# Time-step logits of an SSD layer with the weights stationary, head squares summed on VectorE, and gate outputs evacuated ahead of weight splits, in a three-layer float32 forward pass on one core

## The reference, cut to what matters

```python
# layer 1: short convolution gate, SSD, memory attention (x: 1 x 256 x 2048)
proj = rms_norm(x, norm_w) @ w_in
sc_b, sc_c, sc_v, sc_z, ssd_z, ssd_xbc, ssd_dt, mq, mz = _split(proj, EVEN_SPLITS)
y_a = sc_b * causal_depthwise_conv(sc_c * sc_v, sc_conv_w) * jax.nn.silu(sc_z)
dt = jax.nn.softplus(ssd_dt + ssd_dt_bias)          # 256 x 32: the time steps
y_b = ssd_chunked(xs, dt, -exp(ssd_a_log), bm, cm) + xs * ssd_d
y_b = group_rms_norm(y_b * silu(ssd_z)) * ssd_norm_w     # mean square over 512 columns
y_m = memory_attention(mq, mem_n, w_mk, w_mv) * silu(mz)
x = x + concatenate([y_a, y_b, y_m]) @ w_out
# layer 2: MLA (latent attention), then the first block's final norm
# layer 3: retention, 8 heads of 512 value columns
q, k, v, g = split(rmsnorm(x) @ w_in)
o = scores(q, k) * decay @ v
o = head_norm(o, gain, center=True) * silu(g)       # mean square over 512 columns, per head
x = x + o @ w_out
x = x + square(relu(rmsnorm(x) @ w_up)) @ w_down
return rmsnorm(x)
```

## Time and profile before

| | |
|---|---|
| median of 3 runs | 2830.67 us (2828.84 to 2835.06) |
| profiled execution, its own time | 2829.0 us |
| its span, first to last instruction | 2827.5 us |
| busy: PE, DVE, ACT | 98%, 69%, 50% of the span |
| mean granted TensorE clock | 0.992 of full |

### The profile page before, as it was taken

One profiled execution on the slowest core, in us unless ns is written; L12 is line 12 of the kernel. 1 busy time (PEld: TensorE's weight loads), 2 busy tenths in 40 slices (PEclk: granted clock), 3 DMA queues, 4 the chain that ended last, 5 costly groups with the idle time before them and its releaser, 6 DMA issues.

```text
span 2827.5 us, 46051 instructions
## 1 busy us (share of the span) xinstructions
PE 2759.5 (98%) x15758; PEld 2394.6 (85%) x15758; DVE 1956.2 (69%) x3098; ACT 1412.8 (50%) x2218; POOL 35.4 (1%) x56
## 2 busy tenths in 40 slices
PE   6999999999999899999999999999999999999998
PEld 5888888888888788888888888888888888888887
DVE  5566568878777677777766666666777576675775
ACT  5544345555554555556555544555554444444444
POOL 0000000000000001000000000000000000000000
PEclk9999899999999999999999999999999999999999
DMA  5555354444674334466545555555555555555553
GB/s 231 196 186 185 119 194 157 157 146 144 213 241 162 105 128 159 152 189 200 181 169 177 179 191 186 172 175 171 174 190 185 187 185 187 185 187 185 186 186 112
DMA packets 76349, 495.73 MB, mean 175 GB/s; under 512 B 8544, under 2 KB 8672, under 8 KB 23792
## 3 DMA queue, kind: packets, MB, share of 16 engines
q1 hardware_dynamic: 73568, 478.18, 49.3%
q0 software_dynamic: 2000, 13.70, 1.3%
q10 hardware_dynamic: 704, 2.83, 0.3%
HBM read 486.29 MB, written 8.39 MB: 175 GB/s over the span
## 4 chain that ended last, share of the span: by engine, by line
PE 92%; DVE 3%; ACT 2%; DVEq 2%; issue 1%; DMA 1%; ACTq 0%; POOLq 0%
PE pj L1461 56%; PE pj L1464 28%; PE mx L1478 1%; PE mx L1534 1%; ACT w_hi L405 1%; DVE w_lo L744 1%; PE pj L1570 1%; PE mx L1798 0%; PE mx L1805 0%; DVEq L947 0%; PE mx L1623 0%; PE mx L1738 0%; PE mx L1739 0%; PE mx L1790 0%; PE mx L1611 0%
## 5 line engine op out<-in xcount | busy, mean ns | idle before, releaser
L1461 PE MATMUL pj<-hs,w_hi 128*128 128x512 f32 x4400 | 1564.5, 400 | 4.8 <-DVE xT L758 4.8
L744 DVE TENSOR_TENSOR w_lo<-raw,w_hi 128x1024 fp32r<-128x1024 f32 x1010 | 1136.7, 1130 | 469.3 <-ACT w_hi L405 451.2
L405 ACT ACTIVATE w_hi<-raw 128x1024 fp32r<-128x1024 f32 x1010 | 982.6, 978 | 652.7 <-PE pj L1461 640.2
L1464 PE MATMUL pj<-hs,w_lo 128*128 128x256 f32 x4400 | 1230.1, 280 | 0.0
L1461 PEld LDWEIGHTS pj<-hs,w_hi 128*128 128x128 f32 x4400 | 827.0, 188 | 202.3 <-DVE xT L758 5.1
L1461 PE MATMUL pj<-ys,w_hi 128*128 128x512 f32 x2496 | 885.7, 400 | 8.5 <-DVE ys L809 4.0
L1464 PEld LDWEIGHTS pj<-hs,w_lo 128*128 128x128 f32 x4400 | 830.6, 189 | 3.6 <-issue 2.9
L1464 PE MATMUL pj<-ys,w_lo 128*128 128x256 f32 x2496 | 700.6, 281 | 0.0
L1461 PEld LDWEIGHTS pj<-ys,w_hi 128*128 128x128 f32 x2496 | 471.1, 189 | 126.2 <-DVE ys L809 4.3
L1464 PEld LDWEIGHTS pj<-ys,w_lo 128*128 128x128 f32 x2496 | 473.2, 190 | 0.0
L410 ACT ACTIVATE half<-pj 128x256 f32<-128x256 f32 x491 | 186.6, 380 | 571.8 <-PE pj L1464 559.5
(11 more groups left out here) (279 smaller groups left out, 1411.9 us busy)
## 6 DMA issues: line engine op xcount, KB each, us to landing
raw<-in_w_up SPq DMA_DIRECT2D x64, 1024.0 KB, 4.7
raw<-in_w_down SPq DMA_DIRECT2D x64, 1024.0 KB, 4.8
raw<-in_w_ssd SPq DMA_DIRECT2D x48, 1024.0 KB, 4.7
raw<-in_w_ret_a SPq DMA_DIRECT2D x48, 1024.0 KB, 4.7
raw<-in_w_ret_b SPq DMA_DIRECT2D x48, 1024.0 KB, 4.8
raw<-in_w_out SPq DMA_DIRECT2D x64, 640.0 KB, 3.9
raw<-in_w_gate SPq DMA_DIRECT2D x32, 1024.0 KB, 4.8
raw<-in_w_mem SPq DMA_DIRECT2D x16, 1024.0 KB, 4.9
```

Source lines behind the costliest of these rows:

```text
L405: A(w_hi[:, s, 0:b - a, :], raw[:, c.slot(p, 4), a:b, :], ACT.Copy).then_inc(hi_ready, 1)
L744: TT(w_lo[:, s, 0:b - a, :], raw[:, c.slot(p, 4), a:b, :], w_hi[:, s, 0:b - a, :].bitcast(F32), ALU.subtract).then_inc(split_ready, 1)
L1461: ins = mm(pj[:, k], w_hi[:, s + h, u], m, start=opens and t == 0, stop=False)
L1464: ins = mm(pj[:, k, 0:T], w_lo[:, s + h, u], m[:, 0], start=False, stop=closes and t == order[-1])
```

## The change

1. **dt logits.** The 32 weight columns become hi and lo, padded with zeros to a stationary tile `wd` of 128 x 128 for each of the 16 tiles (made on ACT during `mem` and on DVE ahead of `gate`, in the space of `lat`). 16 matmuls with all 512 columns of `hs` moving give the logits transposed, 64 x 512 raw products. ACT copies them out of PSUM, and six float32 matmuls against columns of the identity (`dt_rows`, ahead of tile 4 of the first output of `gate_out`) turn and add them.
2. **gate_out.** Both steps are written out, not looped. ACT copies an output ahead of the split that stood before it; DVE evacuates and adds ahead of each split. DVE's bias part `dt_in` stands after output 2 and its polynomial `dt_out` after output 3; ACT's exponential stands ahead of its copy of output 3.
3. **ssd.** `mem_scores` moves from after panel 1 to ahead of tile 4 of panel 2, the softmax on DVE and ACT one step later; `stat` from tile 12 to tile 15 of panel 11.
4. **square_sum** moves from tile 11 to 14 in `latent` and `up0`, to 15 in `ret_a`.
5. **Retention.** DVE adds the four squares (128x512, then 128x256); one matmul of 256 columns, ahead of tile 3 of panel 11, takes the place of four after panel 10.

```diff
 # ACT, mem step 1, j == 4
+                        A(wd[:, :, 0:32], wdt[:], ACT.Copy).then_inc(S["dt_split"], 1)
 # ACT, after gate
-            act.wait_ge(S["dt_exp_in"], 1)
-            A(dtw[2], dtw[1], ACT.Exp)
-            A(ea, vec[:, VEC["a_log"][0]:VEC["a_log"][1]], ACT.Exp)
-            act.drain().then_inc(S["dt_exp"], 1)
+            act.wait_ge(S["dt_raw"], 1)
+            A(dtl[0:64], mx[0:64, 1], ACT.Copy).then_inc(S["dt_copied"], 1)
             def gate_out_body(i):
                 for j in range(4):
+                    copy_half("gate_out", i, 2 * j)
                     split("gate_out", i, j, 0)
-                    copy_half("gate_out", i, 2 * j)
+                    if i == 0 and j == 1:
+                        act.wait_ge(S["dt_exp_in"], 1)
+                        A(dtw[2], dtw[1], ACT.Exp)
...
                     copy_half("gate_out", i, 2 * j + 1)
                     split("gate_out", i, j, 1)
 # DVE, ahead of gate
+            v.memset(wd[:, :, 64:128].bitcast(F32), 0.0)
+            dve.wait_ge(S["dt_split"], 1)
+            TT(wd[:, :, 32:64], wdt[:], wd[:, :, 0:32].bitcast(F32), ALU.subtract).then_inc(S["dt_split"], 1)
 # DVE, gate_out
-            residual("gate_out", 1, 2)
+            def gate_out_body(i):
+                for j in range(4):
+                    for u in range(2):
+                        o = 2 * j + u
+                        evac("gate_out", i, o, res[u])
+                        dve.drain()
+                        xo = xT[:, i * 8 + o]
+                        TT(xo, xo, res[u], ALU.add).then_inc(S["x_tile"], 1)
+                        split("gate_out", i, j, u)
+                        if i == 0 and j == 1 and u == 0:
+                            dt_in()
+                    if i == 0 and j == 1:
+                        dt_out()
 # DVE, retention, step j
+                        if j == 10:
+                            dve.wait_ge(S["ret_squares"], i * 1 + (first + 1))
+                            TT(sq_r[:, 0:2], sq_r[:, 0:2], sq_r[:, 2:4], ALU.add)
+                            dve.drain()
+                            TT(sq_r[:, 0], sq_r[:, 0], sq_r[:, 1], ALU.add).then_inc(S["ret_summed"], 1)
 # PE, after gate
-            for r in range(2):
-                for k in range(16):
-                    for part in range(2):
-                        ins = mm(mx[:, 0, 32 * r:32 * r + 32],
-                                 hs[:, k, part, 128 * r:128 * r + 128].bitcast(F32), wdt[:, k],
...
+            for k in range(16):
+                ins = mm(mx[:, 1], wd[:, k], hs[:, k], start=k == 0, stop=k == 15)
+            ins.then_inc(S["dt_raw"], 1)
 # PE, ssd, latent, ret, up0
-                    whole("ssd", i, j, hs, mid={9: yoff} if j == 10 else {12: stat} if j == 11 else {})
+                    whole("ssd", i, j, hs, mid={4: scores} if j == 2 else {9: yoff} if j == 10 else {15: stat} if j == 11 else {})
-                        whole("latent", i, j, hs, {15: (S["h_ready"], 16)}, {11: lambda: square_sum(1)})
+                        whole("latent", i, j, hs, {15: (S["h_ready"], 16)}, {14: lambda: square_sum(1)})
-                            whole(name, i, j, hs)
+                            whole(name, i, j, hs, mid={3: stat} if j == 11 else {})
-                        if j == 10:
-                            pe.wait_ge(S["ret_squares"], i * 1 + (first + 1))
-                            for n in range(4):
-                                ins = mm(mx[:, 5, 0:T], ones, sq_r[:, n], start=n == 0, stop=n == 3)
```

More of the change, by code:

```diff
@@ L470, in mem_body @@
                         hi_columns(17 + 2 * j, hs, "norm0")
+                    if i == 1 and j == 4:
+                        A(wd[:, :, 0:32], wdt[:], ACT.Copy).then_inc(S["dt_split"], 1)
                     if j >= 5:
@@ L905, in _ @@
-            dve.drain()
-            v.reciprocal(den, den)
-            dve.drain()
-            TT(s1, ex, den, ALU.mult)
-            dve.drain()
-            TT(zz, s1, s1, ALU.mult)
-            dve.drain()
-            TS(pp, zz, 1.0 / 15, None, ALU.mult)
-            dve.drain()
-            for k in (13, 11, 9, 7, 5, 3):
-                STT(out=pp, in0=pp, scalar=1.0 / k, in1=zz, op0=ALU.add, op1=ALU.mult)
-                dve.drain()
-            STT(out=pp, in0=pp, scalar=1.0, in1=s1, op0=ALU.add, op1=ALU.mult)
@@ new lines, in dt_out @@
+            def dt_out():
+                dve.wait_ge(S["dt_exp"], 1)
+                TS(den, ex, 2.0, None, ALU.add)
+                dve.drain()
+                v.reciprocal(den, den)
+                dve.drain()
+                TT(s1, ex, den, ALU.mult)
+                dve.drain()
+                TT(zz, s1, s1, ALU.mult)
+                dve.drain()
+                TS(pp, zz, 1.0 / 15, None, ALU.mult)
+                dve.drain()
+                for k in (13, 11, 9, 7, 5, 3):
+                    STT(out=pp, in0=pp, scalar=1.0 / k, in1=zz, op0=ALU.add, op1=ALU.mult)
+                    dve.drain()
+                STT(out=pp, in0=pp, scalar=1.0, in1=s1, op0=ALU.add, op1=ALU.mult)
+                TS(zt, zt, 0.0, None, ALU.max)
+                dve.drain()
+                STT(out=dt, in0=pp, scalar=2.0, in1=zt, op0=ALU.mult, op1=ALU.add)
+                dve.drain()
+                STT(out=da, in0=dt, scalar=-1.0, in1=ea.unsqueeze(1).to_broadcast([P, 2, 32]), op0=ALU.mult,
+                    op1=ALU.mult).then_inc(S["dt_ready"], 1)
@@ L1633, in ydiag, with scores @@
                     ins.then_inc(S["ydiag_ready"], 1)
+                def scores():
+                    pe.wait_ge(evacuated, O(0, 1 + NB))
+                    mem_scores(mq_s, keys[:, i], 3)
                 def yoff():
@@ L1651, in ssd_body @@
                         seg(j - 1)
-                    if j == 1:
-                        pe.wait_ge(evacuated, O(0, 1 + NB))
-                        mem_scores(mq_s, keys[:, i], 3)
                     if j == 5:
@@ L1771, in body, with stat @@
                     O = outputs(name, i)
+                    def stat():
+                        pe.wait_ge(S["ret_summed"], i * 1 + (first + 1))
+                        mm(mx[:, 5, 0:T], ones, sq_r[:, 0], start=True, stop=True).then_inc(S["stat_ready"], 1)
                     for j in range(12):
                         if opening and j == 0:
-                            whole(name, i, j, hs, {15: (S["h_ready"], 32)}, {11: lambda: square_sum(2, 2, rows=True)})
+                            whole(name, i, j, hs, {15: (S["h_ready"], 32)}, {15: lambda: square_sum(2, 2, rows=True)})
                         else:
-                            whole(name, i, j, hs)
+                            whole(name, i, j, hs, mid={3: stat} if j == 11 else {})
                         if 5 <= j <= 8:
@@ L1820, in up_body @@
                         if opening and j == 0:
-                            whole("up0", i, j, hs, {15: (S["h_ready"], 48)}, {11: lambda: square_sum(3)})
+                            whole("up0", i, j, hs, {15: (S["h_ready"], 48)}, {14: lambda: square_sum(3)})
                         else:
```

64 lines of the change are left out of this document (37 added, 27 removed).

## The result

The changed kernel takes 2786.32 us (median of 4, 2782.47 to 2789.06) where the kernel before took 2829.76 beside it (median of 4, 2824.31 to 2835.06): a ratio of 0.9852, 95% interval 0.9839 to 0.9865. That is 43.4 us less. The forecast was 27.7 less, 2803.0 within 2794 to 2812; the result lies 8 us outside the range, on the fast side.

The account below looks back on a forecast made before the run. PE, busy 98% of the span, was taken to bound the kernel. Savings of 14.3 (dt and gate_out), 1.5 and 0.5 (ssd), 2.6 (square_sum) and 8.8 (retention) made 27.7 off the 2830.7 median: 2803.0 us, range 2794 to 2812.

Parts of the forecast that it names:

- One pair of matmuls starts every 0.35 us: PE's matmul pairs: one fixed start distance, 0.35 us, with a panel of 16 pairs taking 5.57.
- other clock drops that a shifted phase can make or unmake, 2 either way: Whole kernel: one of the forecast's own unknowns, clock drops elsewhere from shifted phases, worth 2 us either way.
- tile 14 is 1.04 later, but DVE was busy with a split until then: 0: square_sum in up0: nothing waited there before, so moving the sum to tile 14 saves 0.
- dt: dt logits: 16 full-clock matmuls replace 64, then PE waits for y_gate; saves 17.3 us.
- The rival of a half clock in them: dt logits: the 16 matmuls stay at half clock, 0.43 us each, gate_out begins slow; 2807 us, chance 0.06.
- gate_out: gate_out: saves 2.4 at panel boundaries and 1.7 of half clock; costs dt_rows 1.4, new wait 4.1, clock 1.6.
- the stated bounds of 0 and 3.1: gate_out: limits on the half-clock cost after the new wait, itself taken as 1.6 us.
- ssd and the opening sums: ssd saves 1.5 (stat) and 0.5 (scores), opening sums of latent and ret_a save 2.6: 4.6 us less.
- Retention: Retention heads: three sums fewer in each of 8 save 10.4 us, new ret_out waits cost 1.6; saves 8.8.
- the rival with DVE as the bound: Retention heads: DVE's additions slip its times by 1.2 us per head, the 8.8 vanish; 2812 us, chance 0.12.
- the slower one: Retention, panel 11: a head's sum of squares comes late, PE waits about 5 us per head; 2853 us, chance 0.02.
- the stated unknowns: Forecast's own uncertainties: gate_out wait and clock 0 to 8, ssd 0 to 4.8, other clock drops 2; 2797 to 2809.

Follow-up runs that it names:

- b_up14: Kernel before with only the sum of squares of up0 moved from tile 11 to 14: 2813.14 us against 2828.45, ratio 0.9949.
- a_up11: Changed kernel with the sum of squares of up0 put back at tile 11: 2790.05 us, ratio 0.9857.
- a_cut: Changed kernel with the dt polynomial cut in seven pieces, one behind each split from output 3 of gate_out: 2786.05 us against 2826.98, ratio 0.9851.
- a_lone7: Changed kernel with a lone float32 matmul, result unread, ahead of tile 7 of up0's second panel: 2797.28 us against 2827.55.
- a_lone: Changed kernel with a lone float32 matmul, result unread, ahead of tile 8 of up0's second panel: 2787.05 us, ratio 0.9857.
- b_gate: Kernel before with the dt and gate_out parts alone: 2807.94 us against 2826.98, ratio 0.9931.
- a_again: The changed kernel itself run once more, unmodified, five executions: 2788.13 us against 2828.89, ratio 0.9851.

## Why the forecast was wrong

- **What failed** is the sentence "One pair of matmuls starts every 0.35 us" taken as a constant, and with it the bound "other clock drops that a shifted phase can make or unmake, 2 either way". The rounding hid two values, 0.347 and 0.353. In the earlier trace rows the pairs of ret_out_a start 0.35 apart, and so do those of up and down; only 64 pairs, or a window of 100 us, tell them apart. 1.9% of pair time over the 2048 pairs of up and down is 13.6 us. The step "tile 14 is 1.04 later, but DVE was busy with a split until then: 0" follows from it: right about waits, and by the trace of `b_up14` wrong by 13.5.
- **How the change got the 13.5.** In its trace the wait for `y_ret` had made ret_out_b long, and from there the sum led to short; `a_up11` shows that tile 11 would have done it too. Where ret_out_b came out short, tile 14 kept up0 short in `a_cut` and made it long in `a_lone7`, until the lone matmul. So the gain is partly luck. All nine executions of the change lie below 2790 and seem to have it; that a later one misses it isn't ruled out.
- **The terms themselves** came to 27.5 in the trace where 27.7 stood, but their errors partly cancelled.
- dt: 17.0 for 17.3. The 16 matmuls took full clock and `y_gate` was next to be late, by 1.09. The rival of a half clock in them did not occur.
- gate_out: the waits at the panel boundaries went, and the new one came where it was placed, with the releaser named. It was 2.89 for 4.1, half for each of two reasons: PE came to it 18.7 us after gate_out's begin where 18.1 was reckoned, and the evacuation was done at 21.6 for 22.2, as the polynomial took 4.5 and not 4.9. The clock fell to 0.50 after it, which cost 1.3 for 1.6. How much it costs is a draw: from none to nine pairs at half clock in the seven traces above, so the stated bounds of 0 and 3.1 were right. The Trainium skill's rule of "Why this matters for your kernels" (TensorE: Matmul & The Clock Gate), that an idle gap sends the clock to half, agrees with this wait in five of the seven traces; in `a_lone` and `b_gate` the same wait (2.89 and 3.03) left the clock at 1.00, and the measurement decides.
- ssd and the opening sums: 3.4 together for 4.6. `stat` does not wait, the splits (L753) do, and out0 gives 1.0 back as the last group's chain is DVE's.
- Retention: the heads are shorter by 1.3 to 1.5 each, but for one at 0.7, where 1.3 was forecast, and the ret_out waits cost 0.93 each for 0.8. DVE's additions hid in its idle stretch, and neither the rival with DVE as the bound nor the slower one came near.
- Against the range: the stated unknowns, all taken on the fast side (5.7 in gate_out, 3.3 in ssd, 2 for the clock), come to 11.0 and so to 2792, not to 2797; the result lies beyond that as well. With the terms right and nothing else, the time would have been 2803. The draws in the gate, ret_out_b and memory stages give and take 2 to 5 us, and up and down gave 13.5. In `b_up14` this last one is no chance of the execution: by their times all four runs have it.

## What to carry to other kernels

Where most of the time is one repeated piece, measure its period over hundreds of repetitions in every phase of the program, not from neighbouring starts: 2% of 2500 us is more than most edits, and a period can differ between phases that run the same code. Before crediting an edit with what a comparison shows, count the repetitions per 100 us in stretches that it does not touch, and look at the single executions for two heaps. A serial chain of small DVE operations belongs in pieces between evacuations, not in one block ahead of one.

## What the runs showed of the hardware

- Pairs of matmuls with alternating weights (512 and 256 columns) run at 0.347 or 0.353 us on the average at the full clock, and keep it over as many as 2000 pairs, until something else runs on PE, PE waits, or one start slips (in a head of `a_again` a distance of 370 ns, with no wait in the views, turned 347 347 346 into long). A single float32 matmul of 256 columns (0.43 us) changes the form each time: from long always to short (83 places), from short to short or, where it had 350 and 343 in turn and 350 came last, to long (7 of the 21 places that met short). The difference, 6.7 ns, is 16 cycles of 2.4 GHz; which phase against which clock it is was not found.
- With the same code ahead of it, the gate ran long in some traces and short in others; up and down in the kernel before were long, by its times, in every execution (none of 51 below 2821).
- After waits of 2.89 to 3.03 us at one place of gate_out, none, four or nine pairs ran at half clock (0.64 each), depending on the execution; after 1.09 the pairs of gate_out ran at full clock from the second one on.
